# Reordering copies, roundings and history in the mixers of a two-layer streaming encoder

## The reference

```
for l in (0, 1):
    xn = rmsnorm(x) * g_mix
    qa, ka, va, ga, ra, bb, cb, hb, qc, kc, vc = split(xn @ w_in[l])
    y_a = rmsnorm(gla(qa, ka, va, decays(ga))) * silu(ra)   # chunks of 64, a state per head
    u = cb * hb                                             # short convolution, width 3
    y_b = bb * conv([history(2 columns), u])
    conv_out[l] = last two columns of [history, u]          # an output: 2 x 256, prompt and sample
    y_c = rmsnorm(diff_attention(qc, kc, vc))               # 4 heads, two softmaxes each
    x += [y_a, y_b, y_c] @ w_out[l]
    x += ffn(rmsnorm(x) * g_ffn)      # layer 0: dense swiglu, 2816 wide; layer 1: 2 of 8 experts, 3584 wide
```

## Time and profile before

| | |
|---|---|
| median of 3 runs | 1557.38 us (1557.14 to 1560.73) |
| the profiled execution | 1558.33 us, of which the span of the program's instructions is 1556.5 us |
| TensorE busy | 1536.0 us, 99% of the span |
| VectorE busy | 1238.3 us, 80% |
| ScalarE busy | 998.1 us, 64% |
| GpSimd busy | 218.0 us, 14% |
| moved by DMA | 437.43 MB, mean 281 GB/s |
| layer 0's turns | about 68 to 141 us |
| layer 0's w_out, feed-forward | 149 to 179 us, 179 to 417 us |
| layer 1's turns | about 468 to 542 us |
| experts | from 596 us to 1548 us |

### The profile page before, as it was taken

The page is one execution under the profiler, slowest core; times in us unless marked ns, Lnnn a source line. Parts: engine busy times, 40 slices in busy tenths (PEclk is TensorE's granted clock), DMA queues, the critical chain, the costliest instruction groups (busy, mean ns, idle before and its releaser), DMA issues.

```text
span 1556.5 us, 21546 instructions
## 1 busy us (share of the span) xinstructions
PE 1536.0 (99%) x8398; PEld 1333.7 (86%) x8398; DVE 1238.3 (80%) x1255; ACT 998.1 (64%) x1077; POOL 218.0 (14%) x251
## 2 busy tenths in 40 slices
PE   9999999999999999999999999999999999999998
PEld 7988999999998887888888888888888888888886
DVE  5877576664478658998898898988898898898897
ACT  5555433333356447777777777777777777777775
POOL 5513400000150224102002002002002002002000
PEclk9999999999999999999999999999999999999999
DMA  8432744543443278999999999999999999999994
GB/s 223 122 92 101 145 124 152 163 163 122 143 137 113 82 164 317 403 379 382 379 371 381 382 366 375 393 360 380 389 361 382 384 363 376 398 362 366 393 368 183
DMA packets 159830, 437.43 MB, mean 281 GB/s; under 512 B 12213, under 2 KB 66305, under 8 KB 145393
## 3 DMA queue, kind: packets, MB, share of 16 engines
q1 hardware_dynamic: 151796, 423.02, 75.0%
q0 software_dynamic: 5680, 9.62, 2.5%
q10 hardware_dynamic: 2252, 3.41, 0.8%
HBM read 429.40 MB, written 13.60 MB: 285 GB/s over the span
## 4 chain that ended last, share of the span: by engine, by line
PE 91%; DVE 3%; ACT 3%; DMA 2%; POOL 1%; issue 1%; SPq 0%; DVEq 0%; ACTq 0%; POOLq 0%
PE bank L1951 28%; PE bank L2428 13%; PE bank L2439 13%; PE bank L2432 13%; PE bank L2450 7%; PE bank L2453 7%; PE bank L2459 7%; PE bank L1954 2%; PE bank L2468 2%; DMA ring<-ffn_w_gate 1%; ACT cut_hi L898 1%; DVE cut_lo L1321 1%; DMA gla<-b_g 0%; POOL acc L699 0%; ACT pe L1013 0%
## 5 line engine op out<-in xcount | busy, mean ns | idle before, releaser
L1777 DVE TENSOR_TENSOR split_lo<-raw,split_hi 128x2048 fp32r<-128x2048 f32 x336 | 762.9, 2290 | 99.8 <-ACT split_hi L1184 98.8
L1184 ACT CAST split_hi<-raw 128x2048 fp32r<-128x2048 f32 x336 | 640.6, 1912 | 222.9 <-PE bank L2439 144.1
L2428 PE MATMUL bank<-split_hi,xgT_hi 128*128 128x512 f32 x896 | 291.3, 395 | 0.2 <-ACT xgT_hi L1231 0.2
L2432 PE MATMUL bank<-split_hi,xgT_lo 128*128 128x512 f32 x892 | 285.5, 390 | 0.0
L1321 DVE TENSOR_TENSOR cut_lo<-ring,cut_hi 128x1024 fp32r<-128x1024 f32 x124 | 153.0, 1236 | 113.2 <-ACT cut_hi L898 112.9
L2439 PE MATMUL bank<-split_lo,xgT_hi 128*128 128x512 f32 x896 | 239.9, 390 | 0.0
L898 ACT CAST cut_hi<-ring 128x1024 fp32r<-128x1024 f32 x124 | 129.6, 1048 | 169.6 <-PE bank L1951 168.1
L1951 PE MATMUL bank<-xT_hi,cut_hi 128*128 128x320 f32 x752 | 236.7, 315 | 1.7 <-DVE gR L1732 1.2
L1951 PE MATMUL bank<-xT_hi,cut_lo 128*128 128x320 f32 x752 | 233.3, 310 | 0.0
L1951 PE MATMUL bank<-xT_lo,cut_hi 128*128 128x320 f32 x752 | 231.9, 308 | 0.0
L2439 PEld LDWEIGHTS bank<-split_lo,xgT_hi 128*128 128x128 f32 x896 | 168.1, 188 | 35.0
(11 more groups left out here) (304 smaller groups left out, 1612.4 us busy)
## 6 DMA issues: line engine op xcount, KB each, us to landing
raw<-moe_w_gate SPq DMA_DIRECT2D x112, 1024.0 KB, 8.2
raw<-moe_w_up SPq DMA_DIRECT2D x112, 1024.0 KB, 7.6
raw<-moe_w_down SPq DMA_DIRECT2D x112, 1024.0 KB, 7.3
ring<-w_in SPq DMA_DIRECT2D x15, 1024.0 KB, 5.4
ring<-ffn_w_gate SPq DMA_DIRECT2D x11, 1024.0 KB, 5.6
ring<-ffn_w_up SPq DMA_DIRECT2D x11, 1024.0 KB, 5.5
ring<-ffn_w_down SPq DMA_DIRECT2D x10, 1024.0 KB, 5.1
ring<-w_out SPq DMA_DIRECT2D x8, 1024.0 KB, 5.0
```

What stands on the lines that cost most here:

```text
L1184: return nc.scalar.copy(split_hi[:, i % SR, :], raw_piece(i)).then_inc(hi_ready, 1)
L1777: V.tensor_tensor(split_lo[:, i % SR, :], raw_piece(i), split_hi[:, i % SR, :].bitcast(F32), ALU.subtract).then_inc(lo_ready, 1)
L2428: TE.matmul(o, xgT_hi[:, kk, :], hi[:, w * k + 512 * c:w * k + 512 * c + 512], start=kk == 0, stop=False)
L2432: TE.matmul(o, xgT_lo[:, kk, :], hi[:, w * k + 512 * c:w * k + 512 * c + 512], start=False, stop=False)
```

## The change

- Ring T gets a new job `hist` after the turns. GpSimd copies the eight history columns side by side (`history_columns`, ahead of the statistics of the second tile of attention); TensorE transposes them in one go (`history_T`, right after the turns), ScalarE copies the 8 x 128 result out (behind the first `swish`), and GpSimd stores it with two transfers of four rows of 128 values instead of four transfers of columns. The waits for `cv_out` are for half as many; VectorE waits for them once more ahead of feed-forward's gates.
- ScalarE in turns 1 to 4: the copies out of ring T stand ahead of `hi`. In turns 2 to 4 kd comes ahead of va, on both ScalarE and TensorE and in ring T.
- VectorE: every `lo` from cut 14 to cut 25 is made one turn later; that of 26 after the last `differ`, that of 27 after the second part of `yc_low`, that of 28 after the third. The product with R of ra(2) comes ahead of the two `y_low`.
- Begin of feed-forward: ScalarE's `hi` of 32, 33 and 34 stand between the squares and ahead of the second four `x_hi`. TensorE does `square_sums` in the middle of g(1) and `spread_rstd` in the middle of u(1). In the down projection ScalarE's and VectorE's roundings stand between the blocks of x.

```diff
     for _n in range(HEADS + 2):
+        if _n == HEADS:
+            JOBS["T"].append(("hist", _l))
...
         if _n in (2, 3, 4):
-            JOBS["T"] += [("tok", "va", _l, _n - 2), ("kd", _l, _n - 2)]
+            JOBS["T"] += [("kd", _l, _n - 2), ("tok", "va", _l, _n - 2)]
...
+        hrow, hcol = glaf[0:8, 3 * T:3 * T + P], glaf[:, 3 * T + P:3 * T + P + 8]
...
+            def history_columns(l):
+                pool.wait_ge(RC.free, RC.emptied(("hb", l, 1)))
+                ends = up[:, :, SEQ - CH:T + 4].rearrange("p b (c n) -> p c n b", c=2)[:, :, CH:CH + 2, :]
+                nc.gpsimd.tensor_copy(hcol.rearrange("p (c j b) -> p c j b", c=2, j=2), ends).then_inc(hist_ready, 1)
             def history_out(l):
-                pool.wait_ge(RC.free, RC.emptied(("hb", l, 1)))
-                for dst, a in ((conv_p, SEQ), (conv_s, T + 2)):
-                    for b in range(2):
-                            pool.dma_start(dst[l, 0, :, b * P:b * P + P].rearrange("j p -> p j"), up[:, b, a:a + 2]).then_inc(cv_out, 16)
+                pool.wait_ge(RT.free, RT.emptied(("hist", l)))
+                for i, dst in enumerate((conv_p, conv_s)):
+                    pool.dma_start(dst[l, 0].rearrange("j (b p) -> (j b) p", b=2), hrow[4 * i:4 * i + 4, :]).then_inc(cv_out, 16)
...
                 for what, t in heads_order:
+                    if (what, t) == ("oc", 1):
+                        history_columns(l)
...  (ScalarE, turns)
                     probs(n)
-                    if n:
-                        hi(q0 + Q_FILL + n + 2)
...
                     if n in (0, 1):
                         rows_copy("vc", n + 1, vc)
                         heads_copy("qt", n + 1, qT)
+                    if n in (2, 3, 4):
+                        copy_t(("kd", l, t), kdn[0:rows, t], ...)
+                        rows_copy("va", t, va)
+                    if n:
+                        hi(q0 + Q_FILL + n + 2)
...
-                    if n in (2, 3, 4):
-                        rows_copy("va", t, va)
-                        copy_t(("kd", l, t), kdn[0:rows, t], ...)
...
                 swish(0)
+                act.wait_ge(RT.full, RT.filled(("hist", l)))
+                nc.scalar.copy(hrow, RT.bank(("hist", l))[0:8, 0:P]).then_inc(RT.free, 1)
...  (ScalarE, begin of feed-forward)
                     for o in range(4):
                         x_hi(1, o)
-                    for o in range(4):
-                        x_square(1, o)
                     hi(w0 + 7)
+                    x_square(1, 0)
+                    x_square(1, 1)
                     hi(w0 + 8)
+                    x_square(1, 2)
+                    x_square(1, 3)
+                    hi(w0 + 9)
                     for o in range(4, KB):
                         x_hi(1, o)
-                    hi(w0 + 9)
                     hi(w0 + 10)
...  (ScalarE, down projection)
-                    for o in range(4):
+                    for o in range(0, 4, 2):
                         x_hi(2, o)
-                    for o in range(4):
+                        x_hi(2, o + 1)
+                        hi(DN0 + HALF + o // 2 + 3)
+                    for o in range(0, 4, 2):
                         x_square(2, o)
-                    for m in range(HALF, 2 * HALF - 1):
+                        x_square(2, o + 1)
+                        hi(DN0 + HALF + 2 + o // 2 + 3)
+                    for m in range(HALF + 4, 2 * HALF - 1):
                         hi(DN0 + m + 3)
...  (VectorE)
                 to_rows(("vc", l, 1))
-                lo(q0 + 14)
...
                     if n:
-                        lo(q0 + Q_FILL + n + 2)
+                        lo(q0 + Q_FILL + n + 1)
...
-                lo(q0 + N_IN + 1)
+                lo(q0 + N_IN)
...
                 differ(HEADS - 1)
+                lo(q0 + N_IN + 1)
                 y_gated(0, RS)
                 y_gated(1, RS)
+                by_R(("ra", l, 2), sraT[:, 2], Rb[:])
                 y_low(0, 0, 1, sraT[:, 0:1])
                 y_low(1, 1, 2, sraT[:, 1:2])
-                by_R(("ra", l, 2), sraT[:, 2], Rb[:])
...
-                lo(q0 + N_IN + 2)
...
                 yc_low(0)
                 yc_low(1)
+                lo(w0 + 2)
+                yc_low(2)
                 lo(w0 + 3)
-                yc_low(2)
...
                     dve.wait_ge(v_out, 16 * 2)
+                    dve.wait_ge(cv_out, 16 * 2)
...
-                    x_next(2, 0)
-                    for m in range(HALF, 2 * HALF - 1):
+                    for o in range(0, 4, 2):
+                        residual(2, o)
+                        residual(2, o + 1)
+                        x_lo(2, o)
+                        x_lo(2, o + 1)
+                        lo(DN0 + HALF + o // 2 + 3)
+                    for m in range(HALF + 2, 2 * HALF - 1):
                         lo(DN0 + m + 3)
...  (TensorE)
                     if n in (2, 3, 4):
-                        rows_T("va", n - 2)
                         pe.wait_ge(gk_ready, 2 * l + 1)
                         decayed_T(n - 2)
+                        rows_T("va", n - 2)
...
+                def history_T():
+                    pe.wait_ge(hist_ready, l + 1)
+                    tr(RT.begin(pe, ("hist", l))[0:8, 0:P], hcol, P).then_inc(RT.full, 1)
+                history_T()
...
                     features(RT, ("u", 0))
-                    square_sums(1)
-                    features(RC, ("g", 1))
-                    features(RT, ("u", 1))
-                    spread_rstd(1)
+                    features(RC, ("g", 1), None, lambda: square_sums(1))
+                    features(RT, ("u", 1), None, lambda: spread_rstd(1))
```

17 lines of the change are left out of this document (8 added, 9 removed).

## The result

The kernel after takes 1544.77 us (median of four runs, 1544.37 to 1549.81), the kernel before 1557.26 us in the same series: 12.5 us less, ratio 0.992, 95% interval [0.9905, 0.9935]. The profiled execution took 1544.94 us (span 1543.1), 13.4 us less than that of before.

What follows compares the result with a forecast made beforehand. TensorE was taken as the bound, its waits and a low-clock stretch as the stake. Terms 2.1 + 0.8 + 1.2 + 0.5 - 0.3 + 1.2 + 2.3 + 1.6 = 9.4 us off 1557.38 gave 1548.0 us; 8-in-10 range 1546.0 to 1552.4.

Steps and rivals of the forecast that it cites:

- Two of the signs that were named: Mixers' turn 2: waits for vc and va under 0.5 us; cut 14's low part ending within 0.1 us of TensorE's start.
- Low parts a turn later: Mixers' turns: VectorE's low parts made one turn ahead instead of two, charged nothing, bound 0 to 2 us lost.
- the mixers' 4.3 us in the sum: Gain forecast for both mixers together, which a rival on moving stops, chance 0.10, would give back.
- The sum's own stake: Whole span: TensorE's waits of 8.7 us and a low clock stretch of 1.6 us, 10.3 us in all.
- Turn 2, copies and low part 14 (2.1) and va (0.8): Mixers' turn 2: copies ahead of rounding win 2.1 us, limited by cut 14's low part; kd first wins 0.8 us.
- End of the mixer (1.2 and 0.5): Mixers' ends: product with R ahead of y's low parts wins 1.2 us; rounding moved away from GpSimd's sum wins 0.5.
- the prediction's case of a held sum: Mixer's end: GpSimd's small sum still held by VectorE's following low part of y, making the total 0.5 us less.
- History (-0.3): Mixers, history through TensorE: added transposition costs 0.15 us per layer, 0.3 us in all, bound 0.3 to 0.6.
- Its role as condition: Removing single-element stores ends slow loads (17.3 against 5.5 us); no time by itself, but a condition for the feed-forward step.
- Begin of feed-forward and down projection (1.2, 2.3, 1.6): Earlier roundings win 1.2 us, sums and spread half a feature later 2.3, no clock fall 1.6.
- the lower bound: Low end of the forecast's own range, 1546.6 us: every bound at its best plus 0.8 us for slow first matmuls.
- the forecast's own range: Whole kernel: 1546.6 to 1549.5 us around the forecast of 1548.0 us, chance 0.64.

Runs made afterwards that it cites:

- e9: Kernel before with only VectorE's low parts made a turn later, ScalarE still rounding ahead of its copies: 1551.89 us, ratio 0.9938.
- e6: Kernel before with only the copies of kd and va ahead of ScalarE's rounding and TensorE transposing kd first: 1564.00 us, ratio 1.0027.
- e10: Kernel after with the product with R of the mixer's last columns put back behind the two low parts of y: 1546.69 us, ratio 0.9908.
- e14: Kernel after with ScalarE's copies of va and kd behind its rounding again and TensorE transposing va first: 1545.72 us, ratio 0.9917.
- e4: Kernel after with the history stored by single elements again, four stores per layer, no transposition through TensorE: 1546.42 us, ratio 0.9904.
- e11: Kernel before with the history through TensorE and the new feed-forward order, the mixers' turns old: 1554.49 us, ratio 0.9955.
- e3: Kernel before with only the order in the dense feed-forward, down projection included, changed: 1560.01 us, ratio 0.9995.
- e8: Kernel after with TensorE's sum of squares and spread put back ahead of g(1) and behind u(1): 1547.79 us, ratio 0.9922.
- e7: Kernel before with only the history changed to one transposition through TensorE and two stores of rows per layer: 1557.76 us, ratio 0.9988.
- e1: Kernel before run once more, unchanged: 1561.74 us, ratio 1.0002.
- e5: Kernel after run once more, unchanged: 1546.57 us, ratio 0.9918.
- e13: Kernel after with VectorE's low part of cut 14 back ahead of turn 0, none in turn 1: 1546.12 us, ratio 0.9915.
- e12: Kernel after with vc's rows transposed in mid-feature and cut 14's low part ahead of the decayed keys: 1547.07 us, ratio 0.9907.

## Where the prediction was right and where it failed

The direction, the order of size and most places are as predicted: the waits for va, gla, y_lo, acc and gR are gone, the clock stretch too, the loads behind w_out land in 5.3 to 5.5 us, the experts' stretch is as long as before (595.78 to 1551.66 us and 582.47 to 1538.28 us: 955.9 and 955.8 us). Two of the signs that were named didn't come: 0.8 us are left of the waits for vc, where under 0.5 was forecast, and the low part of cut 14 ends 0.30 us ahead of TensorE's start in layer 0 and holds it for 0.45 us in layer 1.

**The step that failed is "Low parts a turn later", with its "I charge nothing" and a bound of 0 to 2 us lost.** Alone it makes the kernel 9.5 us faster (e9, 1551.89 against 1561.43), of some 14 us for the whole change. The sum still has a term for most of what it does, because it was booked under other edits: under the copies, which alone are a loss (e6), and under the product with R, whose place is worth nothing (e10). That the mixers' 4.3 us in the sum are no further from the 5.5 us that came is in part luck. The total was missed by two things more: the start, which no edit touches, gave 1.7 us in this pair of executions, and the other places gave 2.3 us more than the sum, because stops were priced at their idle time. The sum's own stake, all waits and the clock stretch, was 10.3 us, and 11.7 us came without the start. By step:

- *Turn 2, copies and low part 14 (2.1) and va (0.8).* 3.3 us came. The mechanism was told one-sidedly: copies ahead of the rounding alone make it worse by 3.8 us in layer 0 and 2.5 us in layer 1 (e6, 12-24 and 112-122, mostly clock stretches), the later low parts alone give 2.25 of the 3.3 us (e9), the copies 1.2 on top (e14). In layer 1 the low part of cut 14 is 0.45 us late, within my bound; in layer 0 it is in time.
- *Low parts a turn later (0).* I had looked at it only as a risk: work made ahead of need seemed free. The runs show that it carries the mixers: 2.25 us in turn 2 and 2.4 us at the mixers' ends (e9 against before), and a load that is issued at the end of the stores of single elements (153.96 us, stores 151.13 to 154.04) instead of in their midst (156.41, stores 155.45 to 158.36), so that none stopped TensorE. The feared price was small: 0.45 us for cut 14 in layer 1, nothing elsewhere in the turns. Against the profiled execution of before these come to some 5 us; the rest of e9's 9.5 us I put down to what other executions of the kernel before lose and the profiled one didn't (below), which is inferred from few profiles.
- *End of the mixer (1.2 and 0.5).* 2.3 us came, but not from the edit that I gave 1.2 us: the product's place is worth nothing (e10), the later low parts do it (e9: 1.20 and 1.21 us in 24-28 and 122-126). Which of them, 25 to 28, was not separated. GpSimd's sum is short now (0.19 us, 1.77 before), and its next instruction is longer (1.67 us, 1.16 before). Timeline of GpSimd in the kernel after:

```profile
146.13 0.19 POOL L684 TENSOR_TENSOR small_ss<-small_ss,sm0e 64x4 f32<-64x4 f32 x1 [5.79 <-DVE small_ss L1395]
146.40 1.67 POOL L685 TENSOR_TENSOR small_rs<-small_ss,half_neg 64x4 f32<-64x4 f32 x1
```

  Of the 1.6 us that the sum became shorter, 0.5 went to the next instruction, beside which VectorE's low parts of y run (from 146.36 us on, two of them). The sum itself was over by then, so the prediction's case of a held sum didn't come. That GpSimd is slowed beside VectorE's instructions with two SBUF inputs is what the Trainium skill's GPSIMD Engine Reference, Specifications, says, and this trace agrees. TensorE no longer waits for the chain, so it costs nothing.
- *History (-0.3).* 0.2 us (e4). Its role as condition is right for the old turns alone (e11 against e3), not for the change as a whole.
- *Begin of feed-forward and down projection (1.2, 2.3, 1.6).* 6.1 us came, for 5.1. Sums and spread are 1.9 of it (e8), for the 2.3 booked, and the slow load 0.6 (e7). The clock stretch stayed away as soon as the stop was halved (e8).
- *The size of a stop.* I priced a stop at its idle time. TensorE in the kernel before, around the stop in the down projection:

```profile
388.02 0.31 PE L1951 MATMUL bank<-hT_lo,cut_hi 128*128 128x320 f32 x1
388.16 0.31 PE L1951 MATMUL bank<-hT_hi,cut_lo 128*128 128x320 f32 x1
388.86 0.41 PE L1951 MATMUL bank<-hT_hi,cut_hi 128*128 128x320 f32 x1 [0.39 <-DVE cut_lo L1321]
389.11 0.31 PE L1951 MATMUL bank<-hT_lo,cut_hi 128*128 128x320 f32 x1
```

  Matmuls start 0.15 us apart; here it is 0.70, and then 0.25. A shown idle of 0.39 us costs 0.55 + 0.10 = 0.65 us, which is the column 90-98. The surplus is not the same at every stop: 28-32 gained 0.55 us for 0.39 idle, while the two stops of e8, 1.79 us idle, cost 1.90. Over the stops removed outside turn 2 it comes to about 1.6 of the 2.3 us by which the places other than the start exceed 9.4, by estimate: 2.3 for 1.7 idle at the mixers' ends, 0.55 for 0.39, 4.9 for 2.9 idle and 1.55 of clock in 32-38, 0.65 for 0.39. The other 0.7 are turn 2, 0.4 above its terms, the history, 0.2 less than booked in these columns, and 0.1 of idle time that the terms for the feed-forward left out. I had put 0.8 us for it into the lower bound only.
- *The start (not in the sum).* 1.7 us, chance. The code up to cut 6 is the same in all seventeen profiles, and they take 39.7 to 44.3 us: 39.7 to 41.3 in the ten without a stretch of low clock there, 42.1 to 42.6 in the five with one of 7 us, 43.8 and 44.3 in the two with 10 us, in kernels with the old turns and with the new. The waits of the start are left out in the earlier trace rows, though the prediction calls it the list of the whole span. One of them is this, against 0.5 us in the kernel after:

```profile
PE bank L1954 <- DMA gla<-b_g: 1.9, 1, 1.9
```

- *Small things.* With every bound at its best the terms add up to 9.9 us, not 10.0, and the upper end of the forecast's own range, 1549.5, has no working.

Against the medians the rest is what the one profile of the kernel before didn't show. Of the five profiled executions with the stop of 1.30 us in layer 0 (before, e1, e3, e7, e11), three had a clock stretch behind it, 1.55 us each, and in two (e1, e3) a late load stopped TensorE; in the later series, of 11 to 23 runs each, its median is 1559.7 to 1561.4 us, and the kernel after gains 14 us (1546.57 against 1560.24, e5). The base of 1557.4 us rested on few runs. But the kernel after is 1.8 us slower in e5 than in the first series too, so part of the difference may lie in the chips; this isn't separated.

## What to carry to other kernels

Price a stop of a pipelined engine by the distance between starts, not by the idle time shown. An instruction that is issued earlier than needed is no free lead: it delays what stands behind it in its engine's order (1.2 us of VectorE's here made ScalarE wait 1.90 us and not 0.58), and moving it later can be the gain itself. Two edits that look like one step can be each other's condition (e6) or substitutes (e13, e14); and one profile of a kernel with stops shows one draw of its clock and its loads, so profile it more than once before forecasting to a few microseconds.

## What the runs showed of the hardware

- At the begin of the feed-forward the granted clock fell to 1.2 GHz behind TensorE's stop of 1.2 us for GpSimd's sum in six of six profiles, behind one of 1.62 us there (e3), and behind one of 0.6 us in none of one (e8). Behind the next stop, 1.20 us for gR some ten microseconds later, it fell in none of seven, e8 among them. Behind a stop of 1.30 us in turn 2 it fell in three of five profiles in layer 0 and in none of five in layer 1, and behind one of 1.84 us (e6) in both layers, for 7 us in the first and 3.4 us in the second. So the length of a stop alone doesn't decide it.
- At the lower level matmuls with 320 columns start 0.27 us apart (e9, 184.6 to 187.3 us), at the upper 0.15.
- Three times (e3, e9, e12) it fell in the last turns of a mixer with no stop ahead, where TensorE was busy almost without a gap with many small matmuls (51 in 4.4 us in e9); windows of TensorE in e9 and, with the clock at 1.00 in about the same place of the kernel after, in e5:

```profile
521.00:525.40 4.40, 4.28 (x51) 1.00 0.00 0
525.50:528.90 3.40, 3.40 (x15) 0.50 0.02 5
529.00:533.00 4.00, 4.00 (x38) 1.00 0.71 262
```

```profile
514.00:518.00 4.00, 3.94 (x39) 1.00 0.00 0
518.00:521.50 3.50, 3.44 (x36) 1.00 0.02 5
```

  Each cost about 1.55 us. Why there and not in every execution stays open.
- A store of 1 KB in single elements takes 8.6 us to landing where the load is issued as the last of the four is (e9), and 15.2 us where it is issued among them (e1), medians of four; the load then takes 15.1 and 21.0 us, and 5.2 us without such stores (e7).
